# Expert weights of a hybrid encoder layer: eleven prefetched chunks in a new order of rooms, and 4 MB transfers into pairs of slots

## The reference

```python
def expert_choice_moe(x, w_router, w_gate, w_up, w_down):
    cap = EC_CAPACITY_FACTOR * S // N_EXPERTS            # 64 tokens for each of 16 experts
    logits = jnp.einsum('bsd,de->bse', x, w_router, preferred_element_type=jnp.float32)
    affinity = jax.nn.softmax(logits, axis=-1)
    gates, idx = lax.top_k(jnp.swapaxes(affinity, 1, 2), cap)
    xe = jax.vmap(lambda xb, ib: xb[ib])(x, idx)
    hid = jax.nn.silu(jnp.einsum('becd,edf->becf', xe, w_gate)) * \
        jnp.einsum('becd,edf->becf', xe, w_up)
    ye = jnp.einsum('becf,efd->becd', hid, w_down) * gates[..., None].astype(x.dtype)
    ...                                                  # added back to the tokens' rows
x = layer_norm(DN_ALPHA * x + expert_choice_moe(...), ln3_g, ln3_b)
```

## Time and profile before

| | us |
|---|---|
| median of 3 runs | 1286.04 |
| lowest and highest | 1285.44, 1286.87 |
| the profiled execution | 1284.75 |
| its span, first to last instruction | 1282.9 |
| TensorE busy in it | 1158.1 |

### The profile page before, as it was taken

How to read it: one execution, slowest core, us unless ns; L and a number is a source line. 1 busy time by engine, 2 the same in 40 slices (tenths; PEclk the granted TensorE clock), 3 DMA queues, 4 the chain that set the end, 5 groups by cost and what they waited for, 6 DMA issues and landing times.

```text
span 1282.9 us, 13505 instructions
## 1 busy us (share of the span) xinstructions
PE 1158.1 (90%) x5650; PEld 570.7 (44%) x5650; DVE 270.1 (21%) x483; ACT 183.3 (14%) x338; POOL 118.0 (9%) x59
## 2 busy tenths in 40 slices
PE   9999998999399999999889978997998899789995
PEld 6886776888253343333224322432432243224321
DVE  2012376726800020020002001100200020021114
ACT  4223344143000000000000001000000000000002
POOL 3412324420003000000000000000000000000002
PEclk9999999999799999999999999999999999999998
DMA  9422213047679999999999999999999999999994
GB/s 367 169 96 101 81 72 144 31 195 333 273 278 424 427 427 427 428 428 429 428 428 429 427 430 427 428 429 427 429 429 427 429 428 429 429 426 429 426 426 169
DMA packets 37715, 444.45 MB, mean 346 GB/s; under 512 B 5553, under 2 KB 5809, under 8 KB 10417
## 3 DMA queue, kind: packets, MB, share of 16 engines
q1 hardware_dynamic: 35088, 440.66, 82.0%
q10 hardware_dynamic: 2592, 3.29, 0.7%
HBM read 441.84 MB, written 2.10 MB: 346 GB/s over the span
## 4 chain that ended last, share of the span: by engine, by line
PE 73%; DMA 17%; DVE 6%; ACT 2%; issue 1%; POOL 0%; DVEq 0%; SPq 0%; ACTq 0%
PE bank L1126 25%; DMA ring<-in_w_exp 16%; PE bank L1165 15%; PE bank L1023 5%; PE bank L1175 4%; PE bank L725 2%; PE bank L727 2%; PE bank L730 2%; PE bank L714 2%; ACT yt L670 1%; PE bank L1152 1%; PE bank L1074 1%; PE bank L862 1%; PE bank L864 1%; PE bank L863 1%
## 5 line engine op out<-in xcount | busy, mean ns | idle before, releaser
L1126 PE MATMUL bank<-ring,yt 128*64 128x512 f32 x2048 | 453.3, 595 | 37.8 <-DMA ring<-in_w_exp 37.8
L1126 PEld LDWEIGHTS bank<-ring,yt 128*64 128x64 f32 x2048 | 142.5, 137 | 329.5 <-issue 257.6
L1165 PE MATMUL bank<-ring,yt 128*64 128x512 f32 x928 | 206.6, 596 | 26.7 <-ACT yt L670 20.9
L1165 PEld LDWEIGHTS bank<-ring,yt 128*64 128x64 f32 x928 | 67.0, 137 | 147.6 <-issue 113.9
L1498 DVE TENSOR_TENSOR work<-bank,work 128x512 f32<-128x512 f32 x32 | 22.1, 692 | 422.5 <-PE bank L1126 422.5
L667 ACT ACTIVATE work<-bank 128x512 f32<-128x512 f32 x32 | 19.1, 598 | 534.9 <-PE bank L1126 534.9
L459 POOL TENSOR_TENSOR stat<-stat 128x1 f32<-128x1 f32 x4 | 2.2, 554 | 863.7 <-DVE stat L1527 863.6
L1023 PE MATMUL bank<-yt,res 128*128 128x128 f32 x512 | 62.8, 282 | 13.1 <-DVE yt L1472 13.1
L1023 PEld LDWEIGHTS bank<-yt,res 128*128 128x128 f32 x512 | 59.8, 196 | 25.4 <-DVE xT L1508 15.2
L1508 DVE TENSOR_TENSOR xT<-bank,xT 128x512 f32<-128x512 f32 x56 | 38.7, 691 | 144.2 <-PE bank L1175 144.2
L444 POOL TENSOR_TENSOR piece<-ring,piece 128x1024 fp32r<-128x1024 f32 x23 | 55.1, 2398 | 123.0 <-ACT piece L509 123.0
(11 more groups left out here) (211 smaller groups left out, 1008.5 us busy)
## 6 DMA issues: line engine op xcount, KB each, us to landing
ring<-in_w_exp SPq DMA_DIRECT2D x181, 2048.0 KB, 29.8
ring<-in_dense SPq DMA_DIRECT2D x12, 2048.0 KB, 8.4
ring<-in_w_exp SPq DMA_DIRECT2D x16, 1024.0 KB, 32.9
ring<-in_x_turned SPq DMA_DIRECT2D x8, 256.0 KB, 5.9
res<-in_na_bias SPq DMA_DIRECT2D x1, 2048.0 KB, 23.5
res<-in_x SPq DMA_DIRECT2D x1, 2048.0 KB, 7.7
xT<-in_w_exp SPq DMA_DIRECT2D x1, 2048.0 KB, 13.7
ring<-in_w_exp SPq DMA_DIRECT2D x4, 512.0 KB, 31.8
```

The lines of the kernel that those rows point to most:

```text
L1126: mm = nc.tensor.matmul(bank[2 * g + n % 2][64 * c:64 * c + 64, :], xeT[:, kk, 64 * e:64 * e + 64], exp_rhs(j, first, k, c), start=kk == 0 ...
L1165: mm = nc.tensor.matmul(bank[5][64 * n:64 * n + 64, :], hidT[:, s, 64 * c:64 * c + 64], exp_rhs(j, first, s, n), start=(g, c, s) == (0, 0, ...
```

## The change

Pair 0 gets other rooms. A table says in which slot each chunk lies. Chunk 10 is loaded first, then 0, 1, 3, 5, 6, 7 and 8 into the ring, chunk 4 into `xT`, chunk 9 scattered as before, and chunk 2 in four rows of 512 KB: two into `work` after the mask of the top-k is turned, two into `ln` after the second norm. Chunks 11 and 12 come in halves, each first half as soon as half of the chunk in its slot has been used. Chunk 14 takes `xT` a second time, and the sums start after it.

From pair 1 on the ring is 4 rooms of two slots. One transfer fills a room (two chunks, 32 KB in each partition, and the array in memory is laid out so), issued when both chunks of the room have been used, and TensorE waits for the whole room ahead of the first. The last room of a pair comes as 3 MB and 1 MB. In pair 7 chunks 22 and 23 come in parts as before.

The third norm's gain and shift come as one row each, and after pair 6 four matmuls with ones spread them into PSUM, from where ACT copies them to `ln`.

```diff
+EARLY, IN_XT, SCATTERED = 2, (4, 14), 9
+FIRST_SLOT = {0: 0, 1: 1, 3: 2, 5: 3, 6: 4, 7: 5, 8: 6, 10: 7, 11: 0, 12: 1, 13: 2, 15: 3, 16: 4, 17: 5, 18: 6, 19: 7,
+              20: 0, 21: 1, 22: 2, 23: 3}
+IN_HALVES = (11, 12)
...
+        early = [work[:, 0:1024], work[:, 1024:2048], ln[:, 0, :], ln[:, 1, :]]
...
+            def load_two(j, pair):
+                room, src = exp_room(j), exp_two(pair, j)
+                if j < CPP - 2:
+                    sp.dma_start(room, src).then_inc(two_landed(j), 16)
                     return
-                sp.dma_start(exp_chunk(j, first), exp_src(pair, j)).then_inc(landed, 16)
+                for rows, landed in ((slice(0, 6), half_in), (slice(6, 8), two_landed(j))):
+                    sp.dma_start(room[:, rows], src[:, rows]).then_inc(landed, 16)
...
-            for j in range(EXTRA + EXTRAS, CPP):
-
-                first_lot = j < EXTRA + EXTRAS + SLOTS
-                sp.wait_ge(exp_used, j - SLOTS + 1 - (EXTRAS if first_lot else 0))
+            sp.wait_ge(turned, TN_MASK + 1)
+            for row in (0, 1):
+                sp.dma_start(early[row], exp_src(0, EARLY)[:, row, :]).then_inc(early_in, 16)
+            sp.wait_ge(normed, 2 * TT)
+            for row in (2, 3):
+                sp.dma_start(early[row], exp_src(0, EARLY)[:, row, :]).then_inc(early_in, 16)
+            for j in range(FIRST_LOTS, CPP):
+                if j in IN_HALVES:
+                    sp.wait_ge(half_used, IN_HALVES.index(j) + 1)
+                    load_exp(j, slice(0, 2))
+                    sp.wait_ge(exp_used, USED_FIRST[j] + 1)
+                    load_exp(j, slice(2, 4))
+                    continue
+                sp.wait_ge(exp_used, USED_FIRST[j] + 1)
                 load_exp(j)
+            for a, row in enumerate((ln3_g, ln3_b)):
+                sp.dma_start(ln[0:1, a, :], row).then_inc(ln_in, 16)
             with sp.Fori(1, LAST) as i:
-                for j in range(CPP):
-                    sp.wait_ge(exp_used, i * CPP + (j - SLOTS + 1))
-                    load_exp(j, i, first=False)
...
+                for j in range(0, CPP, 2):
+                    sp.wait_ge(exp_used, i * CPP + (j - SLOTS + 2))
+                    load_two(j, i)
+            for j in range(0, CPP - 2, 2):
+                sp.wait_ge(exp_used, LAST * CPP + (j - SLOTS + 2))
+                load_two(j, LAST)
...
-            pool.wait_ge(exp_used, EXTRA + 1)
+            pool.wait_ge(exp_used, IN_XT[-1] + 1)
...
-            act.wait_ge(normed, 2 * TT)
-            load_ln(ln3_g, ln3_b)
...
+            act.wait_ge(ln_wide, 1)
+            for a in range(2):
+                for n in range(2):
+                    nc.scalar.activation(ln[:, a, 512 * n:512 * n + 512], bank[2 * a + n][:, :], ACT.Copy).then_inc(ln_kept, 1)
...
+            pe.wait_ge(ln_in, 32 * 2 + 16 * 2)
+            for a in range(2):
+                for n in range(2):
+                    mm = nc.tensor.matmul(bank[2 * a + n][:, :], cst[0:1, C_ONE:C_ONE + P], ln[0:1, a, 512 * n:512 * n + 512],
+                                          start=True, stop=True)
+            mm.then_inc(ln_wide, 1)
...
-    return out.reshape(E * CPE, P, SLOT)
+    return out.reshape(E * CPE // 2, 2, P, SLOT).transpose(0, 2, 1, 3).reshape(E * CPE // 2, P, 2 * SLOT)
```

More of the change, by code:

```diff
@@ L26, with place, landings @@
 SLOTS = 8
-FIRST = 3
-EXTRA = 8
-EXTRAS = 2
 CPE = 12
 CPP = 2 * CPE
+EARLY, IN_XT, SCATTERED = 2, (4, 14), 9
+FIRST_SLOT = {0: 0, 1: 1, 3: 2, 5: 3, 6: 4, 7: 5, 8: 6, 10: 7, 11: 0, 12: 1, 13: 2, 15: 3, 16: 4, 17: 5, 18: 6, 19: 7,
+              20: 0, 21: 1, 22: 2, 23: 3}
+FIRST_LOTS = 11
+IN_HALVES = (11, 12)
+RING_AT = 4
+def place(j):
+    return "xT" if j in IN_XT else FIRST_SLOT[j]
+USED_FIRST = {j: max(m for m in range(j) if m not in (EARLY, SCATTERED) and place(m) == place(j))
+              for j in range(FIRST_LOTS, CPP)}
+def landings(j):
+    return sum(2 if m in IN_HALVES else 1 for m in FIRST_SLOT if m <= j and FIRST_SLOT[m] == FIRST_SLOT[j])
 C_ID, C_TRI, C_ONE, C_RANK = 0, 128, 256, 384
@@ L239, in build @@
         exp_in = [sem(f"exp_in{s}") for s in range(SLOTS)]
-        extra_in = [sem(f"extra_in{n}") for n in range(EXTRAS)]
+        two_in = [sem(f"two_in{s}") for s in range(SLOTS // 2)]
+        early_in, xT_in, scattered_in = sem("early_in"), sem("xT_in"), sem("scattered_in")
+        half_used, ln_wide, ln_kept = sem("half_used"), sem("ln_wide"), sem("ln_kept")
         half_in, y_started = sem("half_in"), sem("y_started")
@@ L308, in exp_rhs, with exp_two @@
         def exp_rhs(j, first, k, c):
-            if first and j == EXTRA + 1:
+            if first and j == EARLY:
+                return early[k][:, 512 * c:512 * c + 512]
+            if first and j == SCATTERED:
                 return scattered[k][2][:, 512 * c:512 * c + 512] if k < 3 else scattered[3 + c][2]
             return exp_chunk(j, first)[:, k, 512 * c:512 * c + 512]
-        chunks = experts.rearrange("c p (k n) -> c p k n", k=4)
+        def exp_two(pair, j):
+            return experts[bass.ds(CPP // 2 * pair + j // 2, 1)].rearrange("c p (k n) -> (c p) k n", k=8)
         def exp_src(pair, j):
-            return chunks[bass.ds(CPP * pair + j, 1)].rearrange("c p k n -> (c p) k n")
+            return exp_two(pair, j)[:, 4 * (j % 2):4 * (j % 2) + 4, :]
         def edge_tokens(v):
@@ L394, in _ @@
             sp.wait_ge(mq_lo_split, MQ_GROUPS)
+            load_exp(10)
+            sp.wait_ge(projected, PJ_ROUTER_T + 1)
             load_exp(0)
-            sp.wait_ge(projected, PJ_ROUTER_T + 1)
+            sp.wait_ge(mo_lo_split, MO_GROUPS)
             load_exp(1)
-            sp.wait_ge(mo_lo_split, MO_GROUPS)
-            load_exp(2)
             sp.wait_ge(projected, PJ_MO)
-            for m in range(3, 6):
-                load_exp(m)
+            for j in (3, 5, 6):
+                load_exp(j)
@@ L420, in _ @@
+            for j in range(0, CPP - 2, 2):
+                sp.wait_ge(exp_used, LAST * CPP + (j - SLOTS + 2))
+                load_two(j, LAST)
+            for j in LAST_PARTS:
                 sp.wait_ge(exp_used, LAST * CPP + (j - SLOTS + 1))
-                if j not in LAST_PARTS:
-                    load_exp(j, LAST, first=False)
-                    continue
                 rows = 4 // LAST_PARTS[j]
@@ L1028, in expert_in @@
             def expert_in(i, j, first):
-                if first and EXTRA <= j < EXTRA + EXTRAS:
-                    pe.wait_ge(extra_in[j - EXTRA], 16 * (1 if j == EXTRA else len(scattered)))
-                elif first and j < EXTRA:
-                    pe.wait_ge(exp_in[exp_slot(j, first)], 16)
-                else:
-                    pe.wait_ge(exp_in[exp_slot(j, first)], i * (16 * CPP // SLOTS) + 16 * ((j - EXTRA - EXTRAS) // SLOTS + 2))
+                if first and j == EARLY:
+                    pe.wait_ge(early_in, 16 * len(early))
+                elif first and j == SCATTERED:
+                    pe.wait_ge(scattered_in, 16 * len(scattered))
+                elif first and j in IN_XT:
+                    pe.wait_ge(xT_in, 16 * (IN_XT.index(j) + 1))
+                elif first:
+                    pe.wait_ge(exp_in[FIRST_SLOT[j]], 16 * landings(j))
+                elif j == CPP - 2:
+                    pe.wait_ge(half_in, i * 16)
+                elif j % 2 == 0:
+                    pe.wait_ge(two_landed(j), i * 48 + (16 * (j // SLOTS) - 32))
             def turn_scat(e):
@@ L1117, in pair @@
                                 pe.wait_ge(mix_kept, i * MIX + 2)
+                                if last:
+                                    pe.wait_ge(ln_kept, 4)
                             if j == 1:
@@ L1128, in pair @@
                                                           exp_rhs(j, first, k, c), start=kk == 0, stop=kk == KT - 1)
+                                if first and k == 1 and j < len(IN_HALVES):
+                                    mm.then_inc(half_used, 1)
                             mm.then_inc(exp_used, 1)
```

39 lines of the change are left out of this document (18 added, 21 removed).

## The result

The changed kernel takes 1290.05 us (median of 7 runs, 1287.83 to 1292.73) where the kernel before took 1285.44 (7 runs, 1283.95 to 1287.06). The ratio is 1.0034, 95% interval 1.0025 to 1.0043: 4.4 us slower. The forecast was 1286.1, with a range of 1279.5 to 1294. The measured time lies inside that range, 4 us above the forecast, and outside the 0.2% that count as no change. The profiled execution took 1287.83 (span 1286.0), the fastest of the seven; before, it took 1284.75 (span 1282.9).

What follows compares the result with a forecast made beforehand. The prediction took DMA to bound the kernel, TensorE close behind. First boundary +3.3, tail +3.8 and rate -7.0 gave +0.1 us, 1284.85 for the profiled execution and a forecast of 1286.1 us, range 1279.5 to 1294.

Steps and rivals of the forecast that it cites:

- rival B: Slower: 4 MB rooms bring nothing, first boundary and tail cost 7.1 us, hence 1293.1 us; chance 0.25.
- case A: The forecast itself: no change that can be told, 1283 to 1289 us; chance 0.44.
- The bound: From the first expert pair on, DMA moves 192 chunks back to back and bounds the kernel, TensorE close behind.
- wrong at the root: The prediction's sign of basic failure: DMA is not the bound after the change.
- The first boundary: Into pair 1's second ring round: DMA stands empty some 6 us, the 2.9 us lead is lost, 3.3 us late.
- The later boundaries: Between later pairs: the queue's four rooms, 39 us, keep DMA fed; priced at nothing.
- The rate: From pair 1 on: 78 transfers spared at 0.09 us each, 7.0 us gained, bounds nothing to 14.6.
- The tail: Last pair: chunk 20 must wait for chunk 21's landing, so the end gets 3.8 us longer.
- The spread: Between pairs 6 and 7: four matmuls take 1.9 us, TensorE's idle 1.70 us covers all but 0.2 us.
- C: Faster: larger transfers lose nearly all that separates 428 from 436 GB/s, 1278.5 us, more likely 1283 to 1281; chance 0.24.
- D: Much slower: DMA runs dry at every boundary, about 1298 us; chance 0.07.

Runs made afterwards that it cites:

- spare matmuls: The changed kernel with four unused matmuls before each of the rooms 16 and 18 and three before room 20, pairs 1 to 6: 1299.6 us, ratio 1.0104.
- the rooms alone: The changed kernel with pair 0 and the third norm's load as before, 4 MB rooms from pair 1, no spread: 1286.27 us, ratio 1.0004.
- six rooms a pair: Kernel before, with 4 MB rooms only for chunks 0 to 7 and 10 to 13 of pairs 1 to 6: 1283.29 us, ratio 0.9981.

## Why the prediction was off

That the time lies in the range says little. The range was wide enough to take in rival B, and case A, the favoured one (1283 to 1289, 0.44), did not come. A slowdown of over 0.2% had been given 0.31.

**The bound** was read rightly for pairs 0 to 6: DMA is full but for one hole, and the DMA rows carry the time. It was not followed into pair 7. There TensorE had waited only 0.91 and 0.65 us for chunks 17 and 19, so of a delay only the first 1.6 us or so are absorbed, and the rest shows in the end. The prediction called TensorE at the last boundary "an engine that is not the last to arrive", and said that it would be wrong at the root if DMA weren't the bound after the change. In pair 7 DMA isn't: TensorE waits for no landing there.

**The first boundary** was right: 12.2 us from issue to landing (12.6 predicted), 3.0 us late (3.3). Two slips had no effect. The 7.7 us were read as those of an empty queue, but the chunk before that one landed only at 371.2, 2.4 us after the issue at 368.8. And by the prediction's own terms chunk 12 would be in at 374.1, not 374.6; it was in at 376.0, and chunk 13 took 7.2 us all the same. The spare 1.6 us of queue that rows 3 showed (9.3 against 7.7) meant also that no lead above it could pass; the prediction only said that the lead was used up by the room.

**The later boundaries** at nothing: right, no hole after the first.

**The rate** was right in size for a wrong reason: 6.0 us (the landing of chunk 21 of the last pair went from 3.0 us late to 3.0 us early) against 7.0. The 0.09 us was laid to the transfer; 16 KB rows in 4 MB transfers show that it belongs to the row. The prediction held against this case, rival B, that a long row would have to be cut in two. It is not: 23,716 packets for 35,088.

**The tail** at 3.8 us was right in the kernel without the spread: chunk 20 started 3.8 us ahead of the landing of chunk 21 before, and with it there (1248.64, behind a wait for DMA). From that landing (1248.5) to the end 35.5 us pass there, 3.6 more than before. The terms as measured, 3.0 - 6.0 + 3.6 = 0.6 us, fit the 0.5 us that this kernel takes more than before from chunk 0 of pair 0 to the end. In the changed kernel TensorE was so late that the landing no longer mattered: from it to the end 38.0 us pass, against 31.9.

**The spread** is the step that failed. It was priced at 0.2 us: four matmuls at 1.9 us, less an idle time of 1.7. The row that was used, 16 for 7.7 us, counts instructions, and a float32 matmul call of this kernel shows as two of them; 8 take 3.85 us. (The same count stands in the description of the kernel before: its 16 matmuls for a chunk are 8 calls in the source, its 8 times 2 with the scatter matrix are 8, its 40 of the gather 20.) Then the gather behind them runs 1.4 us longer, on the low clock. That makes 3.65 us in one profile and 5.3 in the other. That the spread brings the low clock about is borne out by the other traces: in all six with the spread at this boundary the granted clock falls to 0.50 inside it or within 1.3 us behind its end, also where TensorE had no long wait before (2 MB transfers, spare matmuls); in the eight without it the gather takes 4.73 us. Why one-row matmuls do this is not shown. The Trainium skill, "TensorE: Matmul & The Clock Gate", section "Why this matters for your kernels", says that a matmul over 32 rows takes as long as one over 128; the rows agree, 0.48 us an instruction for one row (3.85 for 8) as for 128 (7.71 for 16). That part had been allowed for; the count was not. In the medians the spread is 4.4 us with rooms, and without it the changed kernel stands at a ratio of 1.0000. Counted from chunk 0 of pair 0 it is 2.6 and 4.2 us in the two profiles of the changed kernel.

Rooms have a second effect that the prediction didn't mention: one long wait in place of two short ones, after which 32 matmuls take 8.4 to 8.8 us instead of 7.09 in about half of the cases. In pairs 1 to 5 the next wait takes it up. In chunks 20 to 23 of pair 6 it delays the start of pair 7 by 1.6 us. What it costs by itself no run showed. It is small as long as pair 7 still waits for DMA: the three kernels with rooms and without the spread are at ratios of 1.0000 to 1.0004, with 2.2 to 2.6 us between the lowest and the highest run. With rooms and the spread together TensorE has no wait left in pair 7, and the changed kernel's runs lie 4.9 us apart (3.1 before). That both together let every loss of clock through fits this, but it was only argued.

Rival B's time, 1293.1, was nearer than the forecast (3.0 us off against 4.0), but by luck: its mechanism, rooms that bring nothing, is out, since they bring 6.0 us. C and D are out as well.

## What to carry to other kernels

Before a duration is multiplied, look whether the trace's row counts instructions or calls in the source. When DMA is the bound in the middle, price each addition to another engine again for the last stage, where nothing behind it can take up the delay. Longer rows are worth having where the queue is full (0.075 us for 128 rows here), but waiting for two slots at once cost 3.0 us at the one place where the queue ran empty, and 3.6 in the tail, about what the rows brought. Pair transfers up only in places where several are queued. Two executions are compared from a common event, here chunk 0 of pair 0, when a stage ahead of it takes a microsecond or two more in one than in the other.

## What the runs showed of the hardware

A row of 32 KB travels as one packet, and the rate from 600 to 1200 us goes from 428 to 432 GB/s with it; with 14 transfers a pair and rows of 16 KB it stayed at 428. From issue to landing a 2 MB transfer took 7.4 to 8.8 us when DMA had moved nothing for several us (chunk 10 of pair 0: 8.8 before, 8.8 with the rooms alone, 7.4 with six rooms a pair), and 7.2 to 7.7 close behind another. A 4 MB one alone took 12.1 to 12.3. Eight instructions of one-row float32 matmuls took 3.69 to 4.96 us, and the granted clock stood at 0.50, its lower level of 1.2 GHz, in the 2 us behind them, though TensorE was never idle. Waits of 1.9 to 2.7 us between bursts of 7 us were followed by bursts that began or ran in part at that level in some places and not in others (7 of 15 in the changed kernel's first profile, 7 of 14 in its second), at different ones in two executions of the same program. Waits of 1.2 us at each 2 MB chunk were not followed by slow bursts in any of the three kernels with 2 MB transfers alone.
